# A fused decoder layer with seven-product FFN units: VectorE's extra operations set apart inside a unit, x transposed one half ahead, and per-slot waits in the second output pass

## What is computed

```python
D_MODEL, SEQ, D_FF = 2048, 256, 5504

def rmsnorm(x, g):
    y = x * lax.rsqrt(jnp.mean(x * x, axis=-1, keepdims=True) + 1e-6)
    return y * g

def swiglu_ffn(x, w_in, w_out):          # w_in (2048, 11008), w_out (5504, 2048)
    gate, up = jnp.split(x @ w_in, 2, axis=-1)
    return (jax.nn.silu(gate) * up) @ w_out

x = x + 0.5 * swiglu_ffn(rmsnorm(x, ffn1_norm), ffn1_w_in, ffn1_w_out)
x = x + mixer(rmsnorm(x, mix_norm))      # projections, two kinds of attention, w_out
x = x + 0.5 * swiglu_ffn(rmsnorm(x, ffn2_norm), ffn2_w_in, ffn2_w_out)
```

## Time and profile before

| | us |
|---|---|
| median of 3 runs (1916.43 to 1918.49) | 1917.7 |
| the profiled execution, its own time | 1918.52 |
| its span, first to last instruction | 1916.7 |
| TensorE matmul busy | 1831.7 (96%), 8230 matmuls |
| VectorE busy | 1325.9 (69%) |
| ScalarE busy | 1013.2 (53%) |
| mean granted TensorE clock | 0.987 of full speed |

### The profile page before, as it was taken

One profiled execution on the slowest core, in us unless ns is written; L12 is line 12 of the kernel. 1 busy time (PEld: TensorE's weight loads), 2 busy tenths in 40 slices (PEclk: granted clock), 3 DMA queues, 4 the chain that ended last, 5 costly groups with the idle time before them and its releaser, 6 DMA issues.

```text
span 1916.7 us, 20776 instructions
## 1 busy us (share of the span) xinstructions
PE 1831.7 (96%) x8230; PEld 1507.5 (79%) x8230; DVE 1325.9 (69%) x1389; ACT 1013.2 (53%) x1243; POOL 30.7 (2%) x37
## 2 busy tenths in 40 slices
PE   6999999999999999999999999999999999999998
PEld 4777777777988788877777778877777777988787
DVE  2888888888755555355555555788888888855554
ACT  2656556655644454344444444566566566644443
POOL 1000000000000000000000000000000000000000
PEclk8999999999999999799999999999999999999999
DMA  6444555555665454344444544744444555565661
GB/s 243 144 176 176 185 209 205 207 205 186 217 211 182 175 198 153 104 139 147 160 156 155 173 154 146 271 176 176 175 176 178 208 211 210 193 231 187 204 193 54
DMA packets 153648, 347.16 MB, mean 181 GB/s; under 512 B 5824, under 2 KB 14080, under 8 KB 153424
## 3 DMA queue, kind: packets, MB, share of 16 engines
q1 hardware_dynamic: 151520, 340.28, 50.1%
q0 software_dynamic: 1168, 3.97, 0.6%
q10 hardware_dynamic: 864, 1.58, 0.2%
HBM read 343.70 MB, written 3.68 MB: 181 GB/s over the span
## 4 chain that ended last, share of the span: by engine, by line
PE 71%; DVE 20%; issue 3%; DMA 3%; ACT 3%; SPq 0%; DVEq 0%; ACTq 0%
DVE wlo L905 9%; PE bank L489 8%; PE bank L490 8%; PE bank L491 8%; PE bank L425 7%; PE bank L427 6%; PE bank L426 6%; PE bank L369 5%; PE bank L367 5%; PE bank L368 5%; PE bank L415 3%; PE bank L413 3%; PE bank L414 3%; DMA raw<-ffn_w_in 3%; ACT whi L636 2%
## 5 line engine op out<-in xcount | busy, mean ns | idle before, releaser
L905 DVE TENSOR_TENSOR wlo<-raw,whi 128x1024 fp32r<-128x1024 f32 (+1 forms) x692 | 825.0, 1208 | 474.7 <-ACT whi L636 470.9
L636 ACT ACTIVATE whi<-raw 128x1024 fp32r<-128x1024 f32 (+1 forms) x692 | 724.4, 1049 | 688.6 <-PE bank L369 222.0
L425 PE MATMUL bank<-whi,xs 128*128 128x512 f32 (+1 forms) x768 | 305.1, 397 | 49.2 <-DVE wlo L905 49.2
L426 PE MATMUL bank<-wlo,xs 128*128 128x512 f32 (+1 forms) x768 | 300.2, 391 | 0.0
L427 PE MATMUL bank<-whi,xs 128*128 128x512 f32 (+1 forms) x768 | 300.0, 391 | 0.0
L489 PE MATMUL bank<-whi,aw_hi 128*128 128x512 f32 x688 | 269.3, 391 | 7.2 <-DVE wlo L905 7.2
L491 PE MATMUL bank<-whi,aw_lo 128*128 128x512 f32 x688 | 268.7, 391 | 0.0
L490 PE MATMUL bank<-wlo,aw_hi 128*128 128x512 f32 x688 | 268.7, 390 | 0.0
L425 PEld LDWEIGHTS bank<-whi,xs 128*128 128x128 f32 x768 | 147.0, 191 | 92.0 <-issue 58.5
L427 PEld LDWEIGHTS bank<-whi,xs 128*128 128x128 f32 x768 | 146.9, 191 | 29.3
L426 PEld LDWEIGHTS bank<-wlo,xs 128*128 128x128 f32 x768 | 147.2, 192 | 27.3
(11 more groups left out here) (158 smaller groups left out, 1993.5 us busy)
## 6 DMA issues: line engine op xcount, KB each, us to landing
raw<-ffn_w_in SPq DMA_DIRECT2D x160, 1024.0 KB, 7.2
raw<-ffn_w_out SPq DMA_DIRECT2D x84, 1024.0 KB, 5.5
raw<-w_in SPq DMA_DIRECT2D x48, 1024.0 KB, 5.0
raw<-w_out SPq DMA_DIRECT2D x16, 1024.0 KB, 4.9
raw<-ffn_w_in SPq DMA_DIRECT2D x16, 768.0 KB, 5.8
x<-x SPq DMA_DIRECT2D x4, 512.0 KB, 9.5
raw<-ffn_w_out SPq DMA_DIRECT2D x4, 512.0 KB, 3.8
bias_vectors<-bias_vector POOLq DMA_DIRECT2D x1, 1536.0 KB, 7.8
```

The source lines that it names most:

```text
L425: mm(banks[b][:, 0:w], xs[:, k + i, 0, tok], hi, start=starts[b] and k + i == 0, stop=False, skip_group_check=True)
L426: mm(banks[b][:, 0:w], xs[:, k + i, 0, tok], lo, start=False, stop=False, skip_group_check=True)
L636: A(whi[:, h % SLOTS, 0:n_el], src, ACT.Copy).then_inc(weights_hi, 1)
L905: V.tensor_tensor(wlo[:, h % SLOTS, 0:n_el], src, whi[:, h % SLOTS, 0:n_el].bitcast(f32), ALU.subtract).then_inc(weights_lo, 1)
```

## The change

Four edits; no instruction is added or taken away, and no tile or transfer changes its size.

- In the first plain unit the turns of x move: fourth 0 is turned before the unit, and fourths 1, 2 and 3 right after halves 0, 1 and 2. ScalarE and VectorE split the fourths ahead of halves 0, 2, 3 and 4.
- In `unit` VectorE's order is new: `sum_t2` stands between the two halves of G0, `sum_t4` between the two halves of B21, the adds from PSUM are set one by one between halves (X before Z), and `sum_t1` one half later. ScalarE copies `p1s` before both T2 halves, and `act_copy` stands behind B22. TensorE does `act_turn` behind B11 instead of behind T2.
- Piece B21's slot is free once its second low part is written (`weights_lo`), instead of after `sum_t4`.
- Windows 0 to 3 of the second output pass wait for the half that last read their own slot.

```diff
@@ free (SP)
-                        if i in (LOAD["B11"], LOAD["B21"]):
+                        if i == LOAD["B11"]:
                             return sums_done, 4 * ((UNITS - 1) * u + j)
-                        last = {LOAD["B12"]: T3, ...}[i]
+                        last = {LOAD["B21"]: B21, LOAD["B12"]: T3, ...}[i]
@@ plain_unit (TensorE)
-                    if u == 0 and hh % 2 == 0:
-                        x_turn(0, hh // 2)
                     pe.wait_ge(x_ready, 16 * s + 2 * hh + 2)
                     plain(base + hh, 2 * hh, (Z, X), (True, True), w, KT - 1)
+                    if u == 0 and hh < 3:
+                        x_turn(0, hh + 1)
@@ unit (TensorE)
                 form(base + B11, Y, ...)
+                act_turn(u, j - 1)
                 pe.wait_ge(copied, 3 * first + 1)
...
                 form(base + T2, Y, ...)
-                act_turn(u, j - 1)
@@ TensorE, before plain_unit(0)
+            x_turn(0, 0)
@@ act_window_hi (ScalarE)
                 elif c:
-                    act_e.wait_ge(weights_used, OUT[u] + FT)
+                    act_e.wait_ge(weights_used, OUT[u] + min(2 * (ACT_PAIRS - ACT_SLOTS + p) + 2, FT))
@@ plain_unit (ScalarE; the same edit in VectorE's with x_split_lo)
-                    if u == 0 and i in (0, 2, 4, 6):
-                        x_split_hi(0, i // 2)
+                    if u == 0 and i in (0, 2, 3, 4):
+                        x_split_hi(0, max(0, i - 1))
@@ unit (ScalarE)
-                act_e.wait_ge(sums_done, 4 * first + 3)
-                split(base + T2, ...)
                 act_e.wait_ge(weights_used, base + B11 + 2)
                 act_e.wait_ge(act_f_done, 2 * (UNITS * u + j))
                 A(p1s[:, 0:w], Y[:, 0:w], ACT.Copy).then_inc(copied, 1)
-                split(base + T2 + 1, ...)
+                act_e.wait_ge(sums_done, 4 * first + 3)
+                for i in range(2):
+                    split(base + T2 + i, ...)
...
-                act_copy(u, j - 1)
                 loaded(n + LOAD["G1"])
...
                     split(base + B22 + i, ...)
+                act_copy(u, j - 1)
@@ unit (VectorE)
                 split(base + B11 + 1, ...)
+                split(base + G0, ...)
                 sum_t2(u, j)
-                for i in range(2):
-                    split(base + G0 + i, ...)
+                split(base + G0 + 1, ...)
                 for i in range(2):
                     split(base + T2 + i, ...)
-                for i in range(2):
-                    split(base + B21 + i, ...)
+                split(base + B21, ...)
+                sum_t4(u, j)
+                split(base + B21 + 1, ...)
                 for i in range(2):
                     split(base + T3 + i, ...)
-                sum_t4(u, j)
...
```

More of the change, by code:

```diff
@@ L244, in free @@
                             return weights_lo, IN[u] + 2 * i + 2
-                        if i in (LOAD["B11"], LOAD["B21"]):
+                        if i == LOAD["B11"]:
                             return sums_done, 4 * ((UNITS - 1) * u + j)
-                        last = {LOAD["B12"]: T3, LOAD["B22"]: B22, LOAD["G0"]: G0, LOAD["G1"]: G1, LOAD["U0"]: U0, LOAD["U1"]: U0 + 2}[i]
+                        last = {LOAD["B21"]: B21, LOAD["B12"]: T3, LOAD["B22"]: B22, LOAD["G0"]: G0, LOAD["G1"]: G1, LOAD["U0"]: U0, LOAD["U1"]: U0 + 2}[i]
                         return weights_lo, unit_half(u, j) + last + 2
@@ L742, in unit @@
                 A(p1s[:, 0:w], Y[:, 0:w], ACT.Copy).then_inc(copied, 1)
-                split(base + T2 + 1, piece_half(n + LOAD["B11"], 1, w2), w2)
+                act_e.wait_ge(sums_done, 4 * first + 3)
+                for i in range(2):
+                    split(base + T2 + i, piece_half(n + LOAD["B11"], i, w2), w2)
                 loaded(n + LOAD["B21"])
@@ L1021, in plain_unit @@
                 for i in range(2 * IN_HALVES):
-                    if u == 0 and i in (0, 2, 4, 6):
-                        x_split_lo(0, i // 2)
+                    if u == 0 and i in (0, 2, 3, 4):
+                        x_split_lo(0, max(0, i - 1))
                     split(IN[u] + i, piece_half(IN_P[u] + i // 2, i % 2, w2), w2)
@@ L1048, in unit @@
                 split(base + B11 + 1, piece_half(n + LOAD["B11"], 1, w2), w2)
+                split(base + G0, piece_half(n + LOAD["G0"], 0, w2), w2)
                 sum_t2(u, j)
[L1050 to L1051 removed]
+                split(base + G0 + 1, piece_half(n + LOAD["G0"], 1, w2), w2)
                 for i in range(2):
                     split(base + T2 + i, piece_half(n + LOAD["B11"], i, w2), w2)
[L1054 to L1055 removed]
+                split(base + B21, piece_half(n + LOAD["B21"], 0, w2), w2)
+                sum_t4(u, j)
+                split(base + B21 + 1, piece_half(n + LOAD["B21"], 1, w2), w2)
                 for i in range(2):
                     split(base + T3 + i, piece_half(n + LOAD["B12"], i, w2), w2)
[L1058 removed]
                 for i in range(2):
                     split(base + G1 + i, piece_half(n + LOAD["G1"], i, w2), w2)
[L1061 removed]
                 dve.wait_ge(weights_used, base + T3 + 2)
@@ L1064, in unit @@
                 V.tensor_tensor(gset[:, s, 1, 0:w], Y[:, 0:w], gset[:, s, 1, 0:w], ALU.add).then_inc(w_done, 1)
-                split(base + B22 + 1, piece_half(n + LOAD["B22"], 1, w2), w2)
                 for i in range(2):
-                    split(base + T4 + i, tsum[:, i * w2:(i + 1) * w2], w2)
+                    split(base + B22 + i, piece_half(n + LOAD["B22"], i, w2), w2)
+                split(base + T4, tsum[:, 0:w2], w2)
+                dve.wait_ge(weights_used, base + G1 + 2)
+                dve.wait_ge(w_done, first + 1)
+                V.tensor_tensor(gset[:, s, 1, 0:w], X[:, 0:w], gset[:, s, 1, 0:w], ALU.add).then_inc(gate_added, 1)
+                split(base + T4 + 1, tsum[:, w2:2 * w2], w2)
                 split(base + U0, piece_half(n + LOAD["U0"], 0, w2), w2)
@@ L1071, in unit @@
                 V.tensor_tensor(gset[:, s, 0, 0:w], Z[:, 0:w], gset[:, s, 0, 0:w], ALU.add).then_inc(gate_added, 1)
-                dve.wait_ge(w_done, first + 1)
-                V.tensor_tensor(gset[:, s, 1, 0:w], X[:, 0:w], gset[:, s, 1, 0:w], ALU.add).then_inc(gate_added, 1)
                 split(base + U0 + 1, piece_half(n + LOAD["U0"], 1, w2), w2)
+                split(base + U0 + 2, piece_half(n + LOAD["U1"], 0, w2), w2)
                 if j + 1 < UNITS:
                     sum_t1(u, j + 1)
-                split(base + U0 + 2, piece_half(n + LOAD["U1"], 0, w2), w2)
                 split(base + U0 + 3, piece_half(n + LOAD["U1"], 1, w2), w2)
```

3 lines of the change are left out of this document (removed).

## The result

| | before | changed |
|---|---|---|
| median (range), us | 1917.8 (1916.43 to 1918.49) | 1842.55 (1841.97 to 1842.82) |
| ratio, 95% interval | | 0.9608, 0.9591 to 0.9625 |
| span of the profiled execution, us | 1916.7 | 1840.2 |
| mean granted TensorE clock | 0.987 | 0.995 |

A forecast was written before the change was run, and what follows sets the result against it. TensorE, busy 96% of the span, was taken as the bound, its main wait 49.2 us in 24 stalls for VectorE's low splits. Savings 20.0 + 27.1 + 16.7 + 9.7 = 73.5 gave 1844 us against the median; 8-in-10 range 1838 to 1858.

The forecast's parts named there:

- Units, 47.1 us: Seven-product units of both FFNs: 41.69 us a unit instead of 43.71, saving 27.1 us in the first, 20.0 in the second.
- the walk: One seven-product unit, timed step by step in the new order: every half ready in time, smallest margins 0.5, 0.7, 0.9 us.
- the turn costs nothing in its new place: Units, turn ahead of G0: `swiglu` is done at 2.3, 3.1 us before the turn needs it, so no added cost.
- Rivals A and C: Units: A, part of the stall stays, 1860 us, chance 0.10; C, it only moves to T3 or T1, 1891, 0.02.
- The cover for late transfers: Units, ahead of T1: `sum_t1` up to 2.8 us late for its transfers would not reach TensorE.
- rival D: Units: late transfers delay `sum_t1`, slower than before; gain used up at 6.5 us late; 1944 us at 5 a unit; chance 0.01.
- Start, 16.7 us: First plain unit: half 8 starts at 41.4 instead of 58.12 us; gaps of 1.2 and 0.3 us remain.
- Output passes, 9.7 us: Between the output passes: the 3.6 us gap goes in each FFN, plus 2.5 us of slow clock in the first.
- The mixer, 0: Mixer, behind half 8: all as before, only shifted, so no saving.
- rival B: Units and start: the clock's slow stretches stay or new ones come, costing 5 us, 1849 us; chance 0.10.
- the rule of the Trainium skill: First FFN's units: only longer idle gaps are warned of, so both slow stretches would stay, making the time 3.4 us longer.

The follow-up runs named there:

- e4_g0_swap_only: The kernel before with only G0's first low split moved ahead of `sum_t2` on VectorE; 1880.35 us, ratio 0.98.
- e7_t4_back: The changed kernel with `sum_t4` put back behind T3's low splits and B21's slot free only after that sum; 1864.29 us, ratio 0.9716.
- e9_t1_sum_twice: The changed kernel with `sum_t1` computed twice in each unit, making it 2.3 us late without changing transfers; 1862.51 us, ratio 0.9717.
- e10: The changed kernel with ScalarE's and VectorE's splits of x's fourths 1, 2, 3 one to two halves later; 1841.55 us, ratio 0.9608.
- e12: The changed kernel with later start splits of x, the forget gate's matmuls in four pieces and the mixer's turns one half later; 1830.72 us, ratio 0.9558.
- e2_pass_only: The kernel before with only the per-slot wait of the second output pass; 1905.92 us, ratio 0.9937.
- e6_turn_back: The changed kernel with TensorE's turn put back behind T2, VectorE's new order kept; 1843.75 us, ratio 0.961.
- e8_late_transfers: The changed kernel with B22's slot held until T4's second low part, so four pieces are asked for 4.9 us later; 1885.0 us, ratio 0.9824.
- e3_unit_only: The kernel before with only the edits inside the seven-product units, B21's slot freed early included; 1873.09 us, ratio 0.976.
- e1_start_only: The kernel before with only the new turns and splits of x in the first plain unit; 1901.68 us, ratio 0.9917.

## Why the prediction held, and where it did not

**Units, 47.1 us: right, in size and in mechanism.** The pitch is 41.69 us, the two stages 407.7, and the walk agrees with the trace to 0.1 us at every place I looked. e4_g0_swap_only shows that the one split moved ahead of `sum_t2` is enough for 1.78 of the 2.02 us. The prediction's claim that the turn costs nothing in its new place is right with `sum_t4` moved, and e7_t4_back shows what it rests on: without that, 1.1 us a unit would be lost at G1. Rivals A and C did not come.

**The cover for late transfers: wrong.** The step "with 2.8 us to spare ahead of T1 such a late sum no longer reaches TensorE" looked only at the instruction that uses the sum. The low split of B11's second half is behind the sum in VectorE's queue and has the smaller margin; e9_t1_sum_twice put the real cover at 1.2 us. The error cost nothing, since the sum isn't late in the changed kernel: `sum_t1` starts 32.1 us into a unit as the walk had it (1390.82 to a unit's end at 1400.41), and the first two of the pieces asked for from 23.1 on landed 4.85 and 7.00 us after their issue. For the same reason rival D was nearer than I had put it. A gain of 73.5 us would be used up at a sum 1.2 + 3.7 = 4.9 us late, not 6.5.

**Start, 16.7 us: 16.25.** Gaps of 1.2 and 0.3 us were forecast, 1.20 and 0.35 came. Halves 2 and 4 came 0.3 us later than the walk had them, and the four halves after them took 0.18 us more than 4 x 2.72. Behind half 0 no slow stretch was left at the start. That the term fits so well is in part luck. In the seven other runs with this order of x, e10 and e12 left out, half 8 starts at 40.5 to 41.7 us, and in the three with the old order at 58.1 to 58.8, because half 0 quickens sooner or later and, in the old order, the slow stretches behind the gaps fall otherwise; so the term could have read 16.2 to 18.3.

**Output passes, 9.7 us: 10.3.** The gap of 3.6 us went in both FFNs, as e2_pass_only shows alone. For the slow stretch behind the first I had taken 2.5 of at most 3.4 us, and 2.8 came. In the second 0.3 us more than the gap went.

**The mixer, 0: 3.0 us.** "Behind half 8 all is as before, shifted" is true of the order of work but not of the clock: a shift alone changes how long the slow stretch at the forget gate is. This term was left out. The other terms, as measured, sum to 73.65 for 73.5 forecast, so what the spans saved beyond the forecast is this one, and it is luck: e6_turn_back and e7_t4_back, with the same mixer, spent 1.7 and 1.6 us more in it than the changed kernel, and e8_late_transfers 3.2.

**The clock.** The trace of before had slow stretches right behind gaps of 1.97 us. In the changed kernel, with no such gap, none is left behind half 0 but the mixer's and one in the last 4 us. So rival B did not come. Nor is there one in the units of any of the ten other kernels in which these gaps are gone or down to 1.1 us; in e3_unit_only and e4_g0_swap_only the rest of the program is that of before. By the rule of the Trainium skill (TensorE: Matmul & The Clock Gate, "Why this matters for your kernels"), as the prediction applied it, those stretches should have stayed and cost 3.4 us; the measurement decides against it here. e1_start_only shows the same from the other side. It keeps the units' gaps, and two of them were followed by a slow stretch, though other ones than before. Three of them on TensorE's timeline:

```profile
202.23 0.47 PE L425 MATMUL bank<-whi,xs 128*128 128x512 f32 x1 [1.95 <-DVE wlo L906]
...
291.97 0.47 PE L425 MATMUL bank<-whi,xs 128*128 128x512 f32 x1 [1.96 <-DVE wlo L906]
...
380.02 0.69 PE L425 MATMUL bank<-whi,xs 128*128 128x512 f32 x1 [1.95 <-DVE wlo L906]
```

and the stretches behind the first and the last:

```profile
202.00:210.00 8.00, 7.77 (x27) 6.26 (x28) 4.71 (x5) 2.93 (x5) 0.00 (x0) 0.79 0.01 2
...
379.00:387.00 8.00, 6.98 (x24) 5.62 (x25) 5.49 (x5) 3.33 (x4) 0.00 (x0) 0.79 0.01 2
```

## What to carry to other kernels

When an operation that is not urgent stands in an engine's queue, ask which short piece of urgent work right behind it is needed first, and put one such piece ahead; here one split per unit, moved alone, gave 39.4 of the units' 47.1 us. The cover of a late operation is the smallest margin of everything behind it in its queue, plus the idle time met on the way, and not the margin of the instruction that uses its result. Moves that each look free can lean on the same cover, as the turn and `sum_t4` did, so try a group also with one of its members put back.

## What was not expected of the hardware

Equal gaps do not get equal clocks. The gaps of 1.95 to 1.97 us in the first FFN were followed by 3.4 us at 1.2 GHz at 131.64 and 221.55 in the kernel before and at 202.23 and 380.02 in e1_start_only, while others of the same length (291.97) kept the full clock. In the three kernels that have such gaps (before, e1_start_only and e2_pass_only) five of fifteen were followed by a slow stretch. The 3.6 us gap between the second FFN's output passes drew nothing in the kernel before:

```profile
1790.00:1800.00 10.00, 6.40 (x29) 5.21 (x29) 8.92 (x12) 7.50 (x10) 0.00 (x0) 1.00 0.34 105
```

and a slow stretch in e1_start_only, where the program had only been shifted in time:

```profile
1766.00:1780.00 14.00, 10.40 (x39) 8.16 (x39) 9.69 (x13) 7.04 (x9) 0.00 (x0) 0.88 0.25 78
```

The run of 96 small matmuls in the mixer did so in each kernel that kept it whole, for 13.7, 17.1 or 20.5 us, and took 15.2 to 17.9 us. What decides between them these runs do not show. It is not the program alone: executions of the kernel before took 1911 to 1926 us at mean clocks of 0.991 to 0.983, those of the changed kernel 1842.0 to 1842.8. So the gaps cost steadiness as well as time, and two versions of this kernel that differ only in a shift can be 2 us apart.
